# The change-over between two mixers of a hybrid decoder step: work put at other places in the engines' orders

## The chip, the cores and the metric

One core of a Trainium2 chip runs the kernel. Its engines are TensorE (PE), VectorE (DVE), ScalarE (ACT), GpSimd (POOL) and SyncE (SP), which here only issues loads and stores. The metric is the device time of one execution in microseconds; lower is better.

## What is computed

A step of a decoder with two layers, for 512 prompt tokens and 8 sample tokens (520 columns, in two halves of 260). All of it is float32, and each large product is made of three products of high and low parts (high times high, high times low, low times high), so every weight tile needs a "high" copy (ACT) and a "low" remainder (DVE).

```python
h = rmsnorm(y, norm_w[0]);  y = y + ssd_mixer(h)[0]          # layer 0: Mamba-2 SSD, 4 groups, grouped norm, w_out
h = rmsnorm(y, norm_w[1]);  y = y + short_conv_mixer(h)[0]   # layer 1
def short_conv_mixer(h, buf, w_in, conv_w, w_out):
    proj = h @ w_in                                          # (1024, 4 * 2048)
    bg, cg, xin, z = four parts of 2048 columns
    conv, new_buf = causal_dwconv(cg * xin, buf, conv_w)
    return (bg * conv * silu(z)) @ w_out, new_buf
y = rmsnorm(y, final_norm_w)
```

The change-over is the stretch in which the last w_out chunks of layer 0 are added to the residual stream, the sum of squares for layer 1's norm is formed, and layer 1's first tiles are projected.

## The kernel before

The residual stream lies transposed in `xT` (128 x 8 x 520). Each engine runs its own order, written out by hand as a list of calls; semaphores join them. Nothing reorders at run time: an instruction that waits holds all behind it on its engine.

**Layer 0's end on PE.** `out_part(4,'o0',0)` to `out_part(4,'o3',1)` are eight parts of 24 matmuls. They alternate between two PSUM pairs, so each waits (`pair_empty`) until DVE's `residual0` has added the part two before it into `xT` (L1423). Then `first_block` runs four projections of 48 matmuls, IN1 to IN1+3, one for each of z, cg, xin and bg of tile 0 (L2123 again, from `project`). Projection IN1 asks for `hhi` and `hlo` (weighed `xT`, high and low) tile by tile. `token_sums` (L2430) sums the squares over partitions, inside projection IN1+2 before its last two k-tiles. The norm factor r1 is not put into h; it is multiplied in behind the projections on DVE.

**Weights.** SP loads 512 KB chunks into four places of `raw`. `load(n, ...)` waits for the high and low parts of chunk n-2 (same place). `load_part(1,"A22")` and `load_part(1,"A")` use two other places. On ACT, `split(g, what)` makes the high part of the chunk four further on (L624) once PE is done with chunk (g, what); on DVE, `next_low(g, what)` makes the low part (L1238). So `split(3,'l3')` makes chunk (4,'o3'), and `split(4,'o0')` makes chunk IN1, the first of w_in of layer 1.

**The new hidden state.** For each of eight k-tiles: ACT squares `xT` (`x_square`, L915, into `sqb`; tile 0 into `sqs`), makes the weighed high part (`x_weigh0`, L906) and a plain weighed copy (`x_plain`, L1045, into `ybuf`, called h32). DVE makes the low part (`x_low`, L1577) and adds the square up (`add_square`, L1571).

**Layer 1's regular blocks.** `block1(j)` for tiles 1 to 15 makes three of four projections' worth by seven half-size products (P1, P5, P2, P6, P3, P7, P4: 12 matmuls each, L2450) of sums of weight quarters (S1 to S4, DVE `sum_1` to `sum_4`) with sums of h quarters (T1 to T4, `mix`, then `mix_high`, `mix_low`), and two whole chunks Z and G (48 matmuls, L2460). `form_high` (L1121) and `form_low` (L1870) are the high and low parts of these weights. Between products ACT copies PSUM banks away (`snapshot` "s" after P1, "y" after P5, "t" after P6, "u" after P7; L1137); P6 waits for "s", P3 for "y", P7 for "t". `silu_z1(j)` (L1161) is ACT's silu of z, and waits for DVE's product zr (L1959, L1960). L2000 is r2 = -r1 * r1, the first use of the norm factor on DVE.

## Time and profile before

| | us |
|---|---|
| median of 3 runs (892.05 to 894.46) | 893.74 |
| the profiled execution, its own time | 893.7 |
| its span, first to last instruction | 892.0 |
| PE busy | 862.9 (97%) |
| DVE busy | 689.9 (77%) |
| ACT busy | 477.6 (54%) |
| POOL busy | 145.2 (16%) |

Times in the rows are us from the span's start. PE is the engine with the largest share. "idle before <- X" behind a row is the time that the engine stood still ahead of it, and what ended that. Matmuls are pipelined: a row's duration is longer than its distance to the next start.

### The profile page before, as it was taken

To read this page: it belongs to the slowest core of one execution; us is meant where nothing else is said; L and a number is where in the kernel's file an instruction comes from. 1 tells how busy PE (TensorE), PEld (TensorE's weight loads), DVE (VectorE), ACT (ScalarE), POOL (GpSimd) and SP (SyncE) were. 2 spreads that over 40 slices of the span, in tenths; PEclk is the share of its full clock that TensorE was granted. 3 is DMA by queue.
4 is the path that set the end of the run, shared out by engine and by line. 5 is a ranking of instruction groups with operands and counts; after the bars stand their busy time and mean duration, and the time that the engine had idled before them with its cause. 6 is when DMAs were issued, how large, how long until landed. Compare 5 with 4: busy or idle time off the path is not lost.

```text
span 892.0 us, 18650 instructions
## 1 busy us (share of the span) xinstructions
PE 862.9 (97%) x7205; PEld 849.7 (95%) x7205; DVE 689.9 (77%) x1149; ACT 477.6 (54%) x937; POOL 145.2 (16%) x95
## 2 busy tenths in 40 slices
PE   4999999999999999999998999999999999999997
PEld 4999999999999999998998999999999999999996
DVE  4589999969997899987798777777777777774534
ACT  6568668454873576665564444444444444543434
POOL 5404531234143321560000000000000000000000
PEclk9999999999999999999999999999999999999998
DMA  7336636553555436624333333333333333323202
GB/s 173 101 117 196 183 104 194 147 172 118 175 170 163 135 94 212 190 96 126 112 98 96 96 96 95 96 95 96 97 103 104 104 106 104 118 83 110 94 1 96
DMA packets 163023, 108.43 MB, mean 122 GB/s; under 512 B 5000, under 2 KB 155152, under 8 KB 162368
## 3 DMA queue, kind: packets, MB, share of 16 engines
q1 hardware_dynamic: 123876, 76.15, 30.1%
q10 hardware_dynamic: 38756, 30.61, 11.1%
q8 instruction: 58, 0.95, 0.4%
q0 software_dynamic: 304, 0.48, 0.4%
q14 instruction: 29, 0.24, 0.1%
HBM read 95.35 MB, written 12.14 MB: 121 GB/s over the span
## 4 chain that ended last, share of the span: by engine, by line
PE 66%; DVE 13%; issue 4%; ACT 3%; DMA 2%; DVEq 0%; POOLq 0%; POOL 0%; ACTq 0%; SPq 0%
PE pair L2460 19%; PE bank L2450 17%; PE pair L2123 11%; PE pair L2183 6%; PE pair L2393 5%; PE bank L2393 5%; DVE acc L1368 2%; DMA raw<-in_sc_w_in 1%; DVE wlo L1238 1%; DVE ylo L1407 1%; PE bank L2276 1%; PE bank L2261 1%; DVE ybuf L1398 1%; DVE em L1462 1%; PE bank L2293 1%
## 5 line engine op out<-in xcount | busy, mean ns | idle before, releaser
L2123 PE MATMUL pair<-hhi,whi 128*128 128x260 f32 x656 | 135.2, 288 | 0.6 <-DVE acc L1368 0.6
L2123 PE MATMUL pair<-hhi,wlo 128*128 128x260 f32 x656 | 132.5, 284 | 0.0
L2123 PE MATMUL pair<-hlo,whi 128*128 128x260 f32 x656 | 132.2, 283 | 0.0
L2123 PEld LDWEIGHTS pair<-hhi,whi 128*128 128x128 f32 x656 | 101.4, 189 | 2.4 <-DVE acc L1368 1.4
L2123 PEld LDWEIGHTS pair<-hlo,whi 128*128 128x128 f32 x656 | 101.9, 190 | 0.0
L2123 PEld LDWEIGHTS pair<-hhi,wlo 128*128 128x128 f32 x656 | 101.5, 189 | 0.0
L2460 PE MATMUL pair<-hhi,wlo 128*128 128x260 f32 x480 | 96.8, 283 | 0.0
L2460 PE MATMUL pair<-hlo,whi 128*128 128x260 f32 x480 | 96.7, 283 | 0.0
L2460 PE MATMUL pair<-hhi,whi 128*128 128x260 f32 x480 | 96.7, 282 | 0.0
L1121 ACT ACTIVATE whi<-raw 128x1024 fp32r<-128x1024 f32 (+1 forms) x60 | 57.0, 951 | 73.4 <-PE pair L2460 66.4
L624 ACT ACTIVATE whi<-raw 128x1024 fp32r<-128x1024 f32 x60 | 63.1, 1054 | 42.0 <-DMA raw<-in_ssd_w_in 35.6
L1870 DVE TENSOR_TENSOR wlo<-raw,whi 128x1024 fp32r<-128x1024 f32 (+1 forms) x60 | 65.5, 1091 | 23.0 <-ACT whi L1121 22.9
L1238 DVE TENSOR_TENSOR wlo<-raw,whi 128x1024 fp32r<-128x1024 f32 x56 | 70.9, 1274 | 6.9 <-ACT whi L624 6.3
L2460 PEld LDWEIGHTS pair<-hhi,whi 128*128 128x128 f32 x480 | 74.1, 189 | 0.0
L2460 PEld LDWEIGHTS pair<-hhi,wlo 128*128 128x128 f32 x480 | 74.0, 188 | 0.0
L2460 PEld LDWEIGHTS pair<-hlo,whi 128*128 128x128 f32 x480 | 73.8, 188 | 0.0
L539 POOL TENSOR_TENSOR sample<-sample 128x1024 f32<-128x1024 f32 x16 | 48.9, 3059 | 94.1 <-DVE sample L1536 94.1
L1368 DVE SCALAR_TENSOR_TENSOR acc<-pair,colA,acc 128x512 f32<-128x512 f32 (+1 forms) x72 | 54.1, 751 | 6.8 <-ACT acc L751 5.0
L2183 PE MATMUL pair<-yhi,whi 128*128 128x260 f32 x256 | 53.7, 291 | 4.2 <-DVE ylo L1407 2.4
L2450 PE MATMUL bank<-fhi,whi 128*128 128x260 f32 x180 | 51.1, 284 | 2.6 <-ACT sqs L1137 2.6
L2183 PE MATMUL pair<-ylo,whi 128*128 128x260 f32 x256 | 52.1, 285 | 0.0
L2183 PE MATMUL pair<-yhi,wlo 128*128 128x260 f32 x256 | 52.0, 285 | 0.0
(332 smaller groups left out, 2221.9 us busy)
## 6 DMA issues: line engine op xcount, KB each, us to landing
raw<-in_sc_w_in SPq DMA_DIRECT2D x64, 512.0 KB, 5.1
raw<-in_ssd_w_in SPq DMA_DIRECT2D x40, 512.0 KB, 4.0
abc<-a_rows ACTq DMA_DIRECT2D x16, 512.0 KB, 4.3
sample<-in_state_ssm ACTq DMA_DIRECT2D x16, 512.0 KB, 4.3
out_new_ssm_s<-sample ACTq DMA_DIRECT2D x16, 512.0 KB, 5.1
raw<-in_ssd_w_out SPq DMA_DIRECT2D x16, 512.0 KB, 3.9
raw<-in_sc_w_out SPq DMA_DIRECT2D x16, 512.0 KB, 3.8
sample<-bc_rows ACTq DMA_DIRECT2D x4, 1024.0 KB, 6.0
```

Source lines behind the costliest of these rows:

```text
L539: pool.tensor_tensor(tdec, st[:, q % 2, :].rearrange("p (b n) -> p b n", n=NS), bcbc[:, :, 1, :], ALU.mult).then_inc(t2_done, 1)
L624: act.activation(whi[:, slot, :], raw[:, slot % RAW, :], ACT.Copy).then_inc(hi_done, 1)
L1121: act.activation(form_of(whi, j, f), form_src(j, f), ACT.Copy).then_inc(form_hi, 1)
L1238: dve.tensor_tensor(wlo[:, slot, :], raw[:, slot % RAW, :], whi[:, slot, :].bitcast(F32), ALU.subtract).then_inc(lo_done, 1)
L1368: t = dve.scalar_tensor_tensor(acc[:, 0:n], pair[p][:, COL0 - PRE0 + k:COL0 - PRE0 + k + n], cw0(k, tile), acc[:, 0:n], ALU.mult, ALU.add)
L1398: dve.scalar_tensor_tensor(y, y, colB[:, w:w + 1], sqs[:, g, :], ALU.mult, ALU.mult).then_inc(ys_done, 1)
L1870: dve.tensor_tensor(form_of(wlo, j, f), form_src(j, f), form_of(whi, j, f).bitcast(F32), ALU.subtract).then_inc(form_lo, 1)
L2123: mm = pe.matmul(b, w[:, slot, k * P:(k + 1) * P], h[:, k, cols], start=(k == 0 and i == 0), stop=(k == KT - 1 and i == 2))
L2183: mm = pe.matmul(half(p, hb), w[:, slot, k * 256 + part * P:k * 256 + (part + 1) * P], y[:, k, hb * TH:(hb + 1) * TH], start=(k == 0 and i ...
L2393: mm = pe.matmul(bank[2 * i + hb][:, 0:TH], w[:, OUT_SLOT[c % SLOT], kk * 512 + i * P:kk * 512 + (i + 1) * P], y[:, hb * TH:(hb + 1) * TH] ...
L2450: mm = pe.matmul(bank[b][:, 0:TH], form_of(w, j, f)[:, cols], h[:, k, :], start=(first and k == 0 and i == 0), stop=(k == 3 and i == 2), s ...
L2460: mm = pe.matmul(bank[b + hb][:, 0:TH], form_of(w, j, f)[:, k * P:(k + 1) * P], h[:, k, hb * TH:(hb + 1) * TH], start=(k == 0 and i == 0), ...
```

## The change

The number of instructions stays the same; some stand at other places.

- SP: the first two loads of the regular block, A22 and A, are issued behind the first and the second projection chunk, not ahead of all four.
- ACT, layer 0's end: in place of squares in one late group, each k-tile's square follows its weighing, into `thx` for even k and `sqb` for odd k (`square_buf`); the wait of square k for the adds is one step looser. The plain copies of tiles 3 to 7 go to the end, and the `split` calls stand elsewhere.
- DVE, layer 0's end: low parts of w_out's chunks one residual earlier, squares added up as they come, three mixes in a row.
- PE: `token_sums` inside projection IN1+1, not IN1+2.
- ACT and DVE, first block: `mix_high(0)`, `mix_high(2)`, `mix_low(0)` ahead of the norm's roots; in block 1 snapshots "s" and "y" ahead of `silu_z1(1)`.

```diff
@@ SP
-            load_part(1, "A22")
-            load_part(1, "A")
             for m, part in enumerate(PARTS):
                 load(IN1 + m, IN1 + m, w_in1[:, :, part * DI:part * DI + P])
+                if m == 0:
+                    load_part(1, "A22")
+                elif m == 1:
+                    load_part(1, "A")
@@ ACT, x_square
-                if k > 1:
-                    act.wait_ge(xsum_done, 7 * layer + k - 1)
-                act.activation(sqs[:, 0, :] if k == 0 else sqb[:, :], xT[:, k, :], ACT.Square).then_inc(sq_done, 1)
+                if layer == 0 and k > 2:
+                    act.wait_ge(xsum_done, k - 2)
+                elif layer == 1 and k > 1:
+                    act.wait_ge(xsum_done, 7 + k - 1)
+                act.activation(sqs[:, 0, :] if k == 0 else square_buf(layer, k), xT[:, k, :], ACT.Square).then_inc(sq_done, 1)
@@ ACT, block 1
-                silu_z1(j)
+                if j > 1:
+                    silu_z1(j)
                 snapshot(j, "s")
                 snapshot(j, "y")
+                if j == 1:
+                    silu_z1(j)
@@ DVE, layer 0's end (the first of it)
             residual0(3, 'l3', 1)
+            next_low(3, 'l1')
+            next_low(3, 'l2')
             residual0(4, 'o0', 0)
-            next_low(3, 'l1')
+            residual0(4, 'o0', 1)
             x_low(0)
-            residual0(4, 'o0', 1)
-            next_low(3, 'l2')
+            next_low(3, 'l3')
+            x_low(1)
             residual0(4, 'o1', 0)
-            x_low(1)
-            next_low(3, 'l3')
+            add_square(0, 1)
+            next_low(4, 'o0')
             x_low(2)
             residual0(4, 'o1', 1)
@@ PE, first_block
-                    project(IN1 + m, m, ..., None if m else KT, token_sums if m == 2 else None)
+                    project(IN1 + m, m, ..., None if m else KT, token_sums if m == 1 else None)
```

The lines of the kernel are 3 to 8 higher after the change than before: L1238 is L1245, L1423 is L1430, L1577 is L1584, L1571 is L1578, L624 is L629, L915 is L922, L906 is L911, L1045 is L1052, L1121 is L1125, L1137 is L1141, L1161 is L1165.

DVE at layer 0's end, before, from the last residual of (3,'l3') on: `xT` rows are residuals, `wlo` low parts of weights, `hlo` low parts of h.

```order
L1423 TENSOR_TENSOR xT<-xT,pair 128x520 x2
L1238 TENSOR_TENSOR wlo<-raw,whi 128x1024
L1577 SCALAR_TENSOR_TENSOR hlo<-xT,colB,hhi 128x520
L1423 TENSOR_TENSOR xT<-xT,pair 128x520
L1238 TENSOR_TENSOR wlo<-raw,whi 128x1024
L1423 TENSOR_TENSOR xT<-xT,pair 128x520
L1577 SCALAR_TENSOR_TENSOR hlo<-xT,colB,hhi 128x520
L1238 TENSOR_TENSOR wlo<-raw,whi 128x1024
```

The same place after the change:

```order
L1430 TENSOR_TENSOR xT<-xT,pair 128x520
L1245 TENSOR_TENSOR wlo<-raw,whi 128x1024 x2
L1430 TENSOR_TENSOR xT<-xT,pair 128x520 x2
L1584 SCALAR_TENSOR_TENSOR hlo<-xT,colB,hhi 128x520
L1245 TENSOR_TENSOR wlo<-raw,whi 128x1024
L1584 SCALAR_TENSOR_TENSOR hlo<-xT,colB,hhi 128x520
L1430 TENSOR_TENSOR xT<-xT,pair 128x520
L1578 TENSOR_TENSOR sqs<-sqs,sqb 128x520
```

Two low parts moved ahead of the residual of (4,'o0',0), and the residual of (4,'o1',0), the last `xT` row here, moved behind a low part and the second `hlo`.

ACT from the last high part of layer 1's first block on, before: the row `th<-zh` is `silu_z1(1)`, the two rows behind it are snapshots "s" and "y".

```order
L1156 ACTIVATE yhi<-sample 128x1040
L1121 ACTIVATE whi<-raw 128x1024
L1161 ACTIVATE th<-zh 128x520
L1137 ACTIVATE sqs<-bank 128x260
L1137 ACTIVATE yob<-bank 128x260
```

The same place after the change:

```order
L1125 ACTIVATE whi<-sample 128x512
L1125 ACTIVATE whi<-raw 128x1024
L1141 ACTIVATE sqs<-bank 128x260
L1141 ACTIVATE yob<-bank 128x260
L1165 ACTIVATE th<-zh 128x520
```

The two snapshots stand ahead of the silu now.

## Rows read from the trace of the kernel before

**Rows 1.** The page's first part: busy us (share of the span) and instructions.

```profile
PE 862.9 (97%) x7205; PEld 849.7 (95%) x7205; DVE 689.9 (77%) x1149; ACT 477.6 (54%) x937; POOL 145.2 (16%) x95
```

**Rows 2.** Waits of PE, 400 to 480 us: total, times, longest.

```profile
PE bank L2450 <- ACT sqs L1137: 2.6, 1, 2.6
PE pair L2183 <- DVE ylo L1407: 2.0, 1, 2.0
PE pair L2183 <- DVE wlo L1238: 1.1, 1, 1.1
```

**Rows 3.** Windows of PE: length, busy (instructions), granted clock, DMA share, GB/s.

```profile
408.00:411.50 3.50, 3.49 (x17) 0.54 0.00 0
...
475.60:876.00 400.40, 400.40 (x3333) 1.00 0.33 93
```

**Rows 4.** Timeline of PE at the gaps: start, us, operation, count, idle before.

```profile
226.67 1.04 PE L2196 MATMUL bank<-sqs,ones 128*128 128x260 f32 x4
227.55 0.39 PE L2221 MATMUL bank<-turned 128*128 128x128 f32 x2
...
408.01 0.56 PE L2183 MATMUL pair<-yhi,whi 128*128 128x260 f32 x2 [1.99 <-DVE ylo L1407]
...
411.77 0.40 PE L2183 MATMUL pair<-yhi,whi 128*128 128x260 f32 x2
...
426.60 0.40 PE L2183 MATMUL pair<-yhi,wlo 128*128 128x260 f32 x2
428.12 0.47 PE L2183 MATMUL pair<-yhi,whi 128*128 128x260 f32 x2 [1.13 <-DVE wlo L1238]
...
449.54 0.41 PE L2123 MATMUL bank<-hhi,wlo 128*128 128x260 f32 x2
...
451.31 0.40 PE L2123 MATMUL bank<-hlo,whi 128*128 128x260 f32 x2
...
468.25 0.28 PE L2450 MATMUL bank<-hhi,wlo 128*128 128x260 f32 x1
471.16 0.39 PE L2450 MATMUL bank<-fhi,whi 128*128 128x260 f32 x1 [2.63 <-ACT sqs L1137]
...
475.60 0.41 PE L2460 MATMUL pair<-hhi,whi 128*128 128x260 f32 x2
```

**Rows 5.** Timeline of SP: two of its loads.

```profile
414.93 0.37 SPq L377 DMA_DIRECT2D raw<-in_ssd_w_out  x1
...
417.79 0.67 SPq L377 DMA_DIRECT2D raw<-in_sc_w_in  x1
```

**Rows 6.** Chain that ended last, 412 to 456 us: start, us, what.

```profile
417.79 7.05 DMA raw<-in_sc_w_in
...
427.23 0.70 DVE xT L1423
...
445.15 4.00 DMA raw<-in_sc_w_in
```

**Rows 7.** Timeline of ACT at the change-over.

```profile
408.66 1.05 ACT L624 ACTIVATE whi<-raw 128x1024 fp32r<-128x1024 f32 x1
...
418.83 1.06 ACT L624 ACTIVATE whi<-raw 128x1024 fp32r<-128x1024 f32 x1 [1.12 <-DMA raw<-in_ssd_w_out]
...
470.20 0.64 ACT L1161 ACTIVATE th<-zh 128x520 f32<-128x520 f32 x1 [4.78 <-DVE zh L1960]
470.74 0.37 ACT L1137 ACTIVATE sqs<-bank 128x260 f32<-128x260 f32 x1
```

**Rows 8.** Timeline of DVE at the change-over.

```profile
409.61 0.69 DVE L1423 TENSOR_TENSOR xT<-xT,pair 128x520 f32<-128x520 f32 x1
...
449.33 0.70 DVE L1571 TENSOR_TENSOR sqs<-sqs,sqb 128x520 f32<-128x520 f32 x1 [0.17 <-ACT sqb L915]
...
454.34 0.70 DVE L2000 SCALAR_TENSOR_TENSOR sqs<-sqs 128x520 f32<-128x520 f32 x1
...
469.41 0.42 DVE L1959 TENSOR_TENSOR zh<-pair,sqs 128x260 f32<-128x260 f32 x1
```

More of the change, by code:

```diff
@@ L302, in dec_conv, with square_buf @@
             return row[:, SEQ:T]
+        def square_buf(layer, k):
+            return thx[:, :] if layer == 0 and k % 2 == 0 else sqb[:, :]
         def y_tile(g, q):
@@ L1049, in _ @@
             x_weigh0(0)
-            x_plain(0)
-            x_weigh0(1)
-            x_plain(1)
-            split(3, 'l3')
-            x_weigh0(2)
-            x_plain(2)
+            split(3, 'l3')
+            x_weigh0(1)
+            x_square(0, 1)
+            split(4, 'o0')
+            x_weigh0(2)
+            x_square(0, 2)
+            x_plain(0)
             x_weigh0(3)
-            x_plain(3)
+            x_square(0, 3)
+            split(4, 'o1')
             store_state(3, 2)
             store_state(3, 3)
-            split(4, 'o0')
-            x_square(0, 1)
             x_weigh0(4)
-            x_plain(4)
+            x_square(0, 4)
+            x_plain(1)
             x_weigh0(5)
-            x_plain(5)
+            split(4, 'o2')
+            x_square(0, 5)
+            x_plain(2)
             x_weigh0(6)
-            x_plain(6)
-            split(4, 'o1')
+            x_square(0, 6)
             x_weigh0(7)
-            x_plain(7)
-            x_square(0, 2)
-            x_square(0, 3)
-            x_square(0, 4)
-            x_square(0, 5)
-            split(4, 'o2')
+            x_square(0, 7)
             split(4, 'o3')
-            x_square(0, 6)
-            x_square(0, 7)
+            for k in range(3, KT):
+                x_plain(k)
             final_state(3, 3)
@@ L1170, in _ @@
             form_high(1, "Z")
+            mix_high(0)
+            mix_high(2)
             act.wait_ge(stat_mm, GROUPS + 1)
@@ L1175, in _ @@
             load_table(SILU)
-            mix_high(0)
             silu_z1(0)
@@ L1179, in _ @@
             form_high(1, "S1")
+            form_high(1, "S2")
             first_tap1(0)
-            form_high(1, "S2")
-            mix_high(2)
+            mix_high(3)
             form_high(1, "S4")
             form_high(1, "S3")
-            mix_high(3)
             for j in range(1, TILES):
                 form_high(j, "G")
-                silu_z1(j)
+                if j > 1:
+                    silu_z1(j)
                 snapshot(j, "s")
                 snapshot(j, "y")
+                if j == 1:
+                    silu_z1(j)
                 form_high(j, "A22")
@@ L1570, in add_square @@
                     dve.wait_ge(xsum_done, 7 * layer + k - 1)
-                dve.tensor_tensor(sqs[:, 0, :], sqs[:, 0, :], sqb[:, :], ALU.add).then_inc(xsum_done, 1)
+                dve.tensor_tensor(sqs[:, 0, :], sqs[:, 0, :], square_buf(layer, k), ALU.add).then_inc(xsum_done, 1)
             def x_low(k):
@@ L1918, in first_block @@
                 cache_row(0)
+                mix_low(2)
+                weigh_silu(0)
+                form_low(1, "A")
                 dve.wait_ge(proj_done, IN1 + 3)
@@ L1923, in first_block @@
                 dve.tensor_tensor(dec[:, :, PRE1], bank[5][:, SEQ - TH:TH], u[:, SEQ:T], ALU.mult).then_inc(xin_free, 1)
-                weigh_silu(0)
-                form_low(1, "A")
+                mix(3)
                 form_low(1, "S1")
                 conv1(0)
-                mix(3)
+                form_low(1, "S2")
+                mix_low(3)
                 dve.wait_ge(proj_done, IN1 + 4)
@@ L1933, in first_block @@
                 dve.tensor_tensor(yt[:, TH:T], bank[7][:, 0:TH], c2[:, TH:T], ALU.mult).then_inc(bg_free, 1)
-                mix_low(0)
-                form_low(1, "S2")
                 form_low(1, "S4")
-                mix_low(2)
                 form_low(1, "S3")
-                mix_low(3)
             def corner11(j):
@@ L1994, in _ @@
             mix_low(1)
+            form_low(1, "Z")
             dve.wait_ge(xsum_done, 7)
             sum_4(1)
-            form_low(1, "Z")
-            mix(2)
+            mix_low(0)
             dve.wait_ge(rs_done, GROUPS + 1)
@@ L2441, in first_block @@
                         pe.wait_ge(ln_done, GROUPS + 1)
-                    project(IN1 + m, m, bank[2 * m][:, 0:TH], bank[2 * m + 1][:, 0:TH], None if m else KT, token_sums if m == 2 else None)
+                    project(IN1 + m, m, bank[2 * m][:, 0:TH], bank[2 * m + 1][:, 0:TH], None if m else KT, token_sums if m == 1 else None)
             def product(j, what, f, part, b, hi, lo, first):
```

35 lines of the change are left out of this document (17 added, 18 removed).

## The prediction

> **What bounds the kernel now.** Read the busy shares first: TensorE (PE) is busy for 862.9 of 892.0 us [rows 1], so only time in which PE stands idle or runs slowly can be won. Next read whom PE waited for between 400 and 480 us, the stretch that the diff touches: three waits, of 2.6, 2.0 and 1.1 us [rows 2]. From 475.6 to 876 us PE is busy for 400.40 of 400.40 us [rows 3], so whatever PE gains ahead of 475.6 us moves the end by the same amount, as long as nothing later waits.
>
> The price of a gap is best taken from starts, not from idle time. In the steady stretch a matmul takes 400.40 / 3333 = 0.120 us [rows 3], a pair 0.24. The PE timeline [rows 4] then gives:
> - **Gap A**, ahead of out_part(4,'o3',0): the pair at 426.60 makes way at 426.84, the next starts at 428.12: 1.28 us.
> - **Gap B**, at token_sums. Undisturbed, its four passes take 227.55 - 226.67 = 0.88 us. Here the pair at 449.54 makes way at 449.78, and the second pair behind the sums starts at 451.31, so the first at 451.07 in effect: 1.29 - 0.88 = 0.41 us.
> - **Gap C**, ahead of product P6 of the first regular block: 468.25 + 0.12 = 468.37 to 471.16, 2.79 us.
> - A fourth loss, the wait of 1.99 us that ends at 408.01 and the 3.76 us for the 18 matmuls behind it (2.16 at the steady rate), hangs on the group norm and y_low. The diff leaves that order alone.
>
> A, B and C are 4.48 us. A check from the other side: from 408.01 to 475.60 PE issues 8 parts of 24 matmuls, 4 projections of 48, one chunk of 48 and six products of 12, that is 504, 60.5 us at 0.120; with 0.88 for the sums and 1.60 for the slow stretch, 63.0 of 67.6 us, so 4.6 us are lost (the 0.1 more is the refilling of the array behind each gap). I use 4.5.
>
> **The change, part by part.** No instruction is added or removed. What counts is which wait ends last.
>
> *Loads and low parts (gap A).* In the chain [rows 6] DVE's residual add at 427.23 (L1423), which frees the PSUM pair for PE, stands on DVE behind the low part of the first sc_w_in projection chunk. That waits for ACT's high part, and that for the load issued at 417.79, which took 7.05 us: SP issued it behind A22, A and the last ssd_w_out chunk (414.93 [rows 5]). Now both low parts l1 and l2 follow the residual at 409.61 [rows 8], 0.6 us later: the first runs from 410.2 to 411.4, the second to 412.6. The high part of the second is there, ACT having started it at 408.66 for 1.05 us [rows 7]. So the last ssd_w_out chunk is issued at about 411.5 instead of 414.93, and the projection chunk at 412.7 instead of 417.79. The next residual cannot start before 412.5 anyway, when PE ends that part (411.77 + 3 pairs [rows 4]), so the two low parts cost nothing there.
> - ssd_w_out took 3.9 us (414.93 until ACT started on it at 418.83 [rows 5, 7]): now it lands at 415.4. ACT makes its high part from 415.4 to 416.4, ahead of x_weigh0(1), whose input is ready at 416.3, one residual behind PE's 415.4. DVE: x_low(0) to 417.0, low part l3 to 418.1, x_low(1), residual (4,'o1',0) from 418.8 to 419.5. PE wants it at 412.5 + 3 parts of 2.88 = 421.1: 1.6 us of cover.
> - The projection chunk: a lone load took 4.00 us, the one behind three others 7.05 [rows 6]. Landing at 416.7 to 419.7. I take 417, since one chunk stands ahead of it now and not three. High part done at 418.5 (at worst 420.8), low part done at 421.2 (at worst 422.1), x_low(2), residual (4,'o1',1) done at 422.6 (at worst 423.5); PE wants it at 424.0. Then residual (4,'o2',0) at 424.7 to 425.4, against 426.84. Gap A closes: 1.28 us.
> - A22 and A now stand between the projection chunks. Chunk IN1+1 waits for low part l3, so it is issued at 418.2; even at 7.05 us it is there at 425.2, and PE asks for it at 438. IN1+2 and IN1+3 have 20 us. A22 and A are read by the sums, after 428. Each is covered.
> - The same order seen with a rule: A22 was issued 0.4 us behind the ssd_w_out chunk, and this one still took only 3.9 us [rows 5, 7]; a later load took nothing from it. The Trainium skill (DMA: Bandwidth & Descriptors, "Queues, rings and completion order") says that completion is not first-in, first-out per issuing engine. By that rule the projection chunk could end late although A22 now stands behind it, and residual (4,'o1',1) would come at the worst case above; the trace shows no such case.
>
> *Squares (gap B).* With one buffer each square waited for the add before it, and the seventh add ran at 449.33 for 0.70 us [rows 8], 0.25 us too late for PE at 449.78. Now the squares alternate between sqb and thx and follow each x_weigh0, and the last add comes right behind x_low(7). PE ended (4,'o3',1) at 428.12 + 2 x 2.88 = 433.9, now at 432.6; residual, weighing, square, low part and add, each 0.6 to 0.7, are done near 436. PE asks for the sums within projection IN1+1, at 432.6 + 5.8 + 4.3 = 442.7. Cover 6 us; gap B closes: 0.41 us. The plain copies go behind on ACT: the last five, at the residual's 0.7 us each, end near 439.5, so mix(0) starts there instead of earlier; three mixes (1.2 each) and sum_2 end at 443.6. Next on DVE is r2, which needs PE's sums (443.6) and ACT's logs and roots; with two mix_high of 1.0 each ahead of them not before 446. The late copies are covered by that.
>
> *Snapshots (gap C).* P6 waited for snapshot "s" at 470.74, which stood on ACT behind silu_z1(1) at 470.20, and that behind DVE's zr product at 469.41 [rows 7, 8]. DVE reached this so late because from r2 (454.34) on it had 15.1 us of work in a row. Two things are removed. The snapshots go ahead of silu_z1(1). And r2 starts near 447.5 instead of 454.34, since the sums come a projection earlier, with mix_low(0) (1.15 us) done before it; DVE is through by 447.5 + 15.1 - 1.15 = 461.5. PE reaches P6 at 468.37 - 1.28 - 0.41 = 466.7; "s" is taken after P1, at 464, and DVE's S2 and mix_low(0) are ready by 459. Even without the swap the silu would be done at 463.5. Late next is snapshot "t" for P7: silu_z1(1), the high parts A22 and Z (2.3 us together) end by 467.7, P6 at 468.1, "t" at 468.5, P7 at 469.6. Gap C closes: 2.79 us.
>
> **Sum:** 893.7 - 4.5 = 889.2 us. 893.7 is the profiled execution's own time (span 892.0 and 1.7 around it); the median of the runs is 893.74, so nothing is to be shifted.
>
> **The rivals.**
> 1. *A new wait in the output projections.* Residual (4,'o1',0) now stands behind x_low(1), that behind x_weigh0(1), that behind a high part that waits for the ssd_w_out load. If this lands after 417 instead of at 415.4, PE waits. For it: the cover is only 1.4 to 1.6 us at three residuals in a row, and a load took 7.05 us once. Against it: that one had three ahead. It gives back 1 to 2.3 us: 890.2 to 891.5.
> 2. *Gap C closes by half.* If DVE stays late, P7 waits for "t" behind a silu at 470.2 and two high parts, 1.4 us: 890.6. Against it: 5 us of cover.
> 3. *The clock.* Behind the 1.99 us gap the granted clock was 0.54 [rows 3], so mostly at the 1.2 GHz level; behind the 2.63 us gap PE kept its pace (36 matmuls in the 4.44 us from 471.16 to 475.60 [rows 4]), that of 2.4 GHz. A gap of that size costs 1.60 us or nothing. The kept gap may come without it, 887.6, or a small new gap may bring it, 890.8. The Trainium skill (TensorE: Matmul & The Clock Gate, "Part 1: The HAM clock gate") has the gate observe PE independently of when the kernel began; by that rule the same gap may cost in one run and not in the next.
> 4. *Slower than before.* The chain of rival 1 with a very late load: each us of landing beyond 417.0 is one us of PE. Break-even with 893.7 is a landing at 421.5; slower by over 0.3% needs 424.2, 12.7 us after issue, where the slowest load shown took 7.05. At 425 the time would be 897.2.
> 5. *It does nothing*, if PE's path holds something not seen behind these gaps: 893.7. Against it: the 504 matmuls account for all but these 4.6 us.
>
> **How the numbers follow.** Forecast 889.2 (its own range 888.2 to 890.1): 0.66. Rival 1: 0.14. Rival 2: 0.05. Rival 3: 0.08. Rival 4: 0.03. Rival 5: 0.04. The range runs from the lower end of rival 3 to just above rival 1, 887.6 to 891.8, and leaves out under 0.2. A difference of 0.3%, 2.7 us, is about what a measurement of this kernel can tell from no change; the line is 891.0. Faster: 0.66 x 0.95, half of rival 1, nearly all of 2 and 3: 0.80 less a little for scatter, 0.79. Slower 0.03, same 0.18.
>
> **What the changed profile would show.** PE's waits between 400 and 480 us hold only the one of 2.0 us for y_low; the projection chunk is issued near 412.7; the sums stand near 442.7 with no gap; P6 follows P2 directly near 466.7; chunk "G" starts near 471.1 instead of 475.60. I am wrong if PE waits for the xT adds between 421 and 424, or if the low clock stands at another place.

## The result, and the profile after

| | before | after |
|---|---|---|
| median beside each other on one chip, 11 executions each | 892.26 us (891.64 to 895.54) | 888.01 us (885.11 to 890.57) |
| ratio | | 0.9938 [0.9924, 0.9952] |
| profiled execution: its time / its span | 893.7 / 892.0 us | 885.1 / 883.4 us |

The change makes the kernel faster by 0.62%: 0.0062 x 892.26 = 5.5 us, with the interval 4.3 to 6.8 us. The forecast was 4.5 us off 893.7, so 889.2. The direction and the waits that closed were forecast rightly; the gain by the ratio is 1 us larger, though its interval still holds the 4.5. The ratio times the 892.26 of the same chip is 886.7 us, under the lower end of 887.6; the measured median itself, 888.01, lies inside the range. The two medians alone would give a ratio of 0.9952 (4.25 us). The median of before is an unsteady number, because its eleven times fall into two groups (six from 891.64 to 892.26, five from 893.74 to 895.54). The means, 893.26 and 887.91 us, give 0.9940. One execution of e1 below took 1696.29 us, in the slow state, and is in none of the numbers.

The first thing to see is the page's busy list of the changed kernel, against [rows 1]: PE has nearly the same busy time (861.0 against 862.9) in a span 8.6 us shorter.

```profile
span 883.4 us, 18649 instructions
## 1 busy us (share of the span) xinstructions
PE 861.0 (97%) x7205; PEld 848.5 (96%) x7205; DVE 687.1 (78%) x1149; ACT 477.1 (54%) x937; POOL 146.8 (17%) x95
```

PE's waits of the changed kernel between 390 and 480 us, against [rows 2]: of three one is left, the one that the diff does not touch.

```profile
engine line waited for: us in total, times, longest us
PE pair L2190 <- DVE ylo L1414: 2.0, 1, 2.0
```

PE's timeline of the changed kernel (columns: start, duration, engine, line, operation, idle before), at the places of [rows 4]: the last matmul before the kept gap and the first behind it; token_sums; the step into product P6; and the start of chunk G.

```profile
403.48 0.40 PE L2190 MATMUL pair<-yhi,wlo 128*128 128x260 f32 x2
405.89 0.47 PE L2190 MATMUL pair<-yhi,whi 128*128 128x260 f32 x2 [2.01 <-DVE ylo L1414]
...
438.98 0.82 PE L2437 MATMUL bank<-sqs,ones 128*128 128x260 f32 x3
...
462.80 0.28 PE L2457 MATMUL bank<-hhi,wlo 128*128 128x260 f32 x1
462.92 0.28 PE L2457 MATMUL bank<-fhi,whi 128*128 128x260 f32 x1
...
467.26 0.41 PE L2467 MATMUL pair<-hhi,whi 128*128 128x260 f32 x2
```

P6 starts 0.12 us behind the matmul before it, where 2.9 us lay between them [rows 4]. Windows of the changed kernel behind the kept gap and over the steady stretch (columns: stretch, its length, busy time of each engine, then the granted clock, the DMA share and GB/s):

```profile
405.89:409.49 3.60, 3.60 (x30) 3.60 (x31) 3.60 (x6) 1.68 (x3) 0.00 (x0) 1.00 0.00 0
467.30:868.00 400.70, 400.70 (x3336) 400.70 (x3335) 277.44 (x479) 168.20 (x287) 0.00 (x0) 1.00 0.33 93
```

Behind the same 2.0 us gap PE now runs at a granted clock of 1.00, the 2.4 GHz level, where before it was 0.54 [rows 3].

**Where the 8.6 us between the two spans are.** I cut each record at PE starts: up to the first matmul behind the 2.0 us gap; from there to chunk G of the first regular block; from there to the last output projection; the rest. (Starts from the PE timelines, before rounding, so that a difference of the printed rows can be 0.01 off; G is at 475.60 before [rows 4] and 467.26 after.)

| record | to the end of the 2.0 us gap | from there to chunk G | G to last projection | rest | low clock behind these gaps |
|---|---|---|---|---|---|
| before | 408.01 | 67.59 | 402.62 | 13.75 | the 2.0 us gap |
| after | 405.89 | 61.38 | 402.62 | 13.48 | neither |

- The second column fell by 6.21 us. The slow 18 matmuls behind the gap cost 1.60 by the prediction's reckoning from [rows 3]; between records of the changed kernel below, the difference is 1.53 us. Without it 4.68 remain, where the three gaps had been sized at 4.48 and the cross-check by 504 matmuls had said 4.6.
- The first column fell by 2.12 us, in a stretch that the change leaves alone. It is scatter: in the records below it ends anywhere from 405.5 to 409.0, for kernels of either order.
- The steady stretch is the same to 0.01 us, so what PE gains ahead of G does move the end.

So one profile against another (8.6 us) says half as much again as the change is worth. The timed executions say 5.5 us (4.3 to 6.8). The question for the experiments is the 1 us between that and the gaps, of which the interval alone does not say that it is there.

### The profile page after: what moved, and what is told of

Its sections match the earlier page's. It is cut to its first block, busy times and chain, and to the rows that moved or that the text cites. A ratio compares the mean times of both kernels' runs of the same rounds, so it can differ in the third digit from the quotient of the medians.

```text
span 883.4 us, 18649 instructions
## 1 busy us (share of the span) xinstructions
PE 861.0 (97%) x7205; PEld 848.5 (96%) x7205; DVE 687.1 (78%) x1149; ACT 477.1 (54%) x937; POOL 146.8 (17%) x95
## 4 chain that ended last, share of the span: by engine, by line
PE 74%; DVE 8%; issue 3%; ACT 2%; DMA 1%; POOLq 0%; DVEq 0%; POOL 0%; ACTq 0%
PE pair L2467 20%; PE bank L2457 17%; PE pair L2130 14%; PE pair L2190 8%; PE pair L2400 5%; PE bank L2400 5%; DVE acc L1375 2%; PE bank L2130 1%; PE bank L2283 1%; PE bank L2268 1%; DVE wlo L1245 1%; DVE ybuf L1405 1%; DVE em L1469 1%; PE bank L2030 1%; DMA abc<-a_rows 1%
## 5 line engine op out<-in xcount | busy, mean ns | idle before, releaser
L1125 ACT ACTIVATE whi<-raw 128x1024 fp32r<-128x1024 f32 (+1 forms) x60 | 57.1, 951 | 78.5 <-PE pair L2467 71.5
L629 ACT ACTIVATE whi<-raw 128x1024 fp32r<-128x1024 f32 x60 | 63.2, 1053 | 40.2 <-DMA raw<-in_ssd_w_in 35.2
L1245 DVE TENSOR_TENSOR wlo<-raw,whi 128x1024 fp32r<-128x1024 f32 x56 | 70.9, 1273 | 1.9 <-ACT whi L629 1.2
L2457 PE MATMUL bank<-flo,whi 128*128 128x260 f32 x180 | 51.0, 283 | 0.0
```

Of the source, the lines that this page charges most:

```text
L629: act.activation(whi[:, slot, :], raw[:, slot % RAW, :], ACT.Copy).then_inc(hi_done, 1)
L1125: act.activation(form_of(whi, j, f), form_src(j, f), ACT.Copy).then_inc(form_hi, 1)
L1245: dve.tensor_tensor(wlo[:, slot, :], raw[:, slot % RAW, :], whi[:, slot, :].bitcast(F32), ALU.subtract).then_inc(lo_done, 1)
L2457: mm = pe.matmul(bank[b][:, 0:TH], form_of(w, j, f)[:, cols], h[:, k, :], start=(first and k == 0 and i == 0), stop=(k == 3 and i == 2), s ...
```

## The experiments

Three theories for what lies beyond the gaps. **Theory 1:** low clocks behind gaps; with fewer and shorter gaps fewer executions get one. **Theory 2:** the change removed something that the prediction had not seen. **Theory 3:** the scatter ahead of 408 us alone. Beside them each step of the prediction is tried for itself. All were timed in three sets (e, f and g), each set on one chip beside the kernel before. (The expectation of f1 calls scatter inside the change-over theory 2, that of g1 calls "no drop, only scatter" theory 3.)

| kernel | median us | ratio to before | us from the first matmul behind the 2.0 us gap to G | low clock behind the 2.0 us gap / gap C |
|---|---|---|---|---|
| e1 changed, again | 887.52 | 0.9924 [0.9899, 0.9950] | 62.91 | yes / no gap |
| f1 changed, again | 887.58 | 0.9942 [0.9921, 0.9964] | 62.94 | yes / no gap |
| e2 changed, no swap | 888.55 | 0.9934 [0.9912, 0.9956] | 62.92 | yes / no gap |
| e3 before + swap | 891.11 | 0.9972 [0.9959, 0.9985] | 65.67 | yes / no |
| e4 changed, old loads | 889.19 | 0.9950 [0.9930, 0.9969] | 63.66 | yes / no gap |
| f4 changed, sums late | 888.39 | 0.9950 [0.9932, 0.9969] | 61.45 | no / no gap |
| f3 before + low parts | 893.79 | 1.0008 [0.9992, 1.0023] | 68.02 | yes / yes |
| g2 the same, again | 892.36 | 0.9999 [0.9982, 1.0015] | 66.50 | no / yes |
| g1 before, again | 893.30 | 1.0008 [0.9992, 1.0025] | 66.83 | no / yes |
| f2 changed + early y tile | 886.36 | 0.9930 [0.9909, 0.9951] | (see there) | no / no gap |
| g3 changed, loads later | 888.00 | 0.9951 [0.9933, 0.9968] | 62.90 | yes / no gap |
| g4 both | 886.66 | 0.9938 [0.9915, 0.9960] | (see there) | no / no gap |

### The changed kernel again (e1, f1)

No edit.

> The changed kernel again, beside the kernel before on one chip, for the part of the gain that the sum does not explain (about 5.5 us measured, 4.5 us summed). Theory 1: the gaps A, B and C are worth 4.5 us, and the rest is TensorE's clock: fewer stretches at the low level in the changed kernel. Then the two kernels' executions, sorted by their mean granted clock, differ by 4.5 us at equal clock (a difference of 0.001 of mean clock is 0.9 us), and the changed kernel's mean clock is higher by about 0.001. Theory 2: the rest lies in a fourth gap that closed too; then the two differ by 5.5 us at equal clock, and a PE timeline aligned matmul by matmul shows a further step between 400 and 480 us. Theory 3: the rest is scatter of the stretch before 400 us, where both kernels have the same orders; then the gain here is anything from 3.5 to 6.5 us.

> The changed kernel once more, beside the kernels of this call. Theory 1 (the three gaps give 4.7 us, and beyond them only the clock drop behind the 2.0 us gap at layer 0's end comes and goes): 0.5 to 0.7% under before, and the stretch from that gap to the chunk G of the first block at 61.4 us without a low clock in it or 62.9 us with it, never between. Theory 2 (scatter of the whole program hides a part of the change elsewhere): that stretch varies by itself, by more than 0.2 us around the two values.

Measured: 62.91 and 62.94 us from the gap's end to G, where the first record had 61.38. The one difference is the clock behind the gap: the PE row and window of f1, the window's fourth number being the granted clock.

```profile
407.29 0.48 PE L2190 MATMUL pair<-yhi,whi 128*128 128x260 f32 x2 [2.00 <-DVE ylo L1414]
```

```profile
408.10:411.50 3.40, 3.40 (x19) 0.51 0.02 5
```

The same gap, in the same kernel: 0.51 here, 1.00 there. It costs 1.53 to 1.56 us or nothing, and in all seven records of the changed order with the 2.0 us gap (after, e1, f1, e2, e4, f4, g3) the stretch had one of these two values (in e4 with the wait shown below on top), never one between. Theory 2 finds no place in the change-over: before and after differ there by the gaps and by low clocks. Theory 3 is true of single records (405.9 to 408.4 us for the first column), but it touches kernels of both orders alike, so it can't move a ratio of medians by itself.

### The swap of the snapshots (e2, e3)

In the changed kernel the swap undone, and in the kernel before the swap alone:

```diff
@@ e2: ACT, block 1 of the changed kernel
-                if j > 1:
-                    silu_z1(j)
+                silu_z1(j)
                 snapshot(j, "s")
                 snapshot(j, "y")
-                if j == 1:
-                    silu_z1(j)
@@ e3: the same edit, the other way, in the kernel before
```

> The changed kernel with one part undone: in block 1, silu_z1(1) stands ahead of the snapshots s and y again. My theory: the early norm factor alone brings DVE to zr by 463 us, so the silu is done before P1 ends and the swap is worth nothing: within 0.3 us of the changed kernel, PE with no wait ahead of P6. Rival: the swap is what closed gap C: 2.8 us slower than the changed kernel, P6 waiting for snapshot s behind the silu.

> The kernel before with the swap alone: snapshots s and y ahead of silu_z1(1). Nothing else moved. Theory: P6 no longer waits, but P7 then waits for snapshot t, which stands behind the silu (zr at about 470 us) and two high parts, for 1.4 to 1.7 us: a gain of 1.2 to 1.4 us on the kernel before. Rival: if the snapshot order was the cause of the whole gap C, the gain is 2.8 us and no wait is left at P7.

e2: 62.92 us against 62.91 with the swap. Once the norm factor comes early the swap is worth nothing, as the prediction's step on gap C said ("even without the swap"). e3: alone, it moves the wait from P6 to P7. PE's waits of e3, and PE and ACT around P7:

```profile
PE pair L2186 <- DVE ylo L1410: 2.0, 1, 2.0
PE bank L2453 <- ACT sqs L1137: 1.2, 1, 1.2
PE pair L2186 <- issue: 0.6, 1, 0.6
```

```profile
470.08 0.28 PE L2453 MATMUL bank<-hhi,wlo 128*128 128x260 f32 x1
471.57 0.39 PE L2453 MATMUL bank<-fhi,whi 128*128 128x260 f32 x1 [1.22 <-ACT sqs L1137]
```

```profile
469.14 0.64 ACT L1161 ACTIVATE th<-zh 128x520 f32<-128x520 f32 x1 [2.70 <-DVE zh L1963]
469.69 1.56 ACT L1121 ACTIVATE whi<-raw 128x512 fp32r<-128x512 f32 x2
471.15 0.36 ACT L1137 ACTIVATE sqs<-bank 128x260 f32<-128x260 f32 x1
```

The chain of rival 2 is there as it was written: silu, two high parts, snapshot "t", P7. It costs 471.57 - 470.08 - 0.12 = 1.37 us, where the prediction said 1.4. The swap alone wins half of gap C, 1.42 us; the other 0.5 us of e3's gain in this record is a smaller gap A (0.6 against 1.1 us in the list of waits), which the swap does not touch.

The timed executions of e3 gain more than the 1.2 to 1.4 us that I expected: 0.28%, 2.5 us (1.3 to 3.7). Their mean granted clock is 0.9928, against 0.9908 for before in the same set. So the wait of 2.6 us that became one of 1.2 us seems to have taken its low clock with it. None stands behind the 1.2 us wait in this record. It is the first sign of what the section on the low parts shows.

### The sums one projection later (f4)

```diff
@@ PE, first_block of the changed kernel
-    project(..., token_sums if m == 1 else None)
+    project(..., token_sums if m == 2 else None)
```

> The changed kernel with PE's token sums back inside projection IN1+2, one projection (5.8 us) later. The prediction said that gap C closes because the norm factor comes a projection earlier, and that the swap of the snapshots is not needed. It also said that DVE would be through its 15.1 us behind r2 by 461.5, 5 us ahead of PE; with the sums 5.8 us later it would be through near 467 and the snapshot s, which now stands ahead of the silu, does not wait for that chain. So theory (either edit alone holds gap C closed for P6): no wait for s, at most 0.5 us at P7 for t, and a time within 0.6 us of the changed kernel. Rival (the early sums carry gap C by themselves): a wait of 1 to 1.5 us at P7 as in the swap alone, and the ratio to before 0.0015 higher than the changed kernel's.

61.45 us, against 61.38 of the record that likewise had no low clock; no wait but the kept one. So gap C is held closed twice over: by the swap with late sums (f4), and by the early sums without the swap (e2). With neither, in the kernel before, it is open. The time, 888.39 against 887.58 us of the changed kernel in the same set, has overlapping intervals.

### The order of the loads (e4, g3)

e4 puts A22 and A back ahead of the projection chunks; g3 puts both behind the second one.

```diff
@@ e4: SP, the changed kernel
+            load_part(1, "A22")
+            load_part(1, "A")
             for m, part in enumerate(PARTS):
                 load(IN1 + m, IN1 + m, ...)
-                if m == 0:
-                    load_part(1, "A22")
-                elif m == 1:
-                    load_part(1, "A")
@@ g3: SP, the changed kernel
-                if m == 0:
-                    load_part(1, "A22")
-                elif m == 1:
-                    load_part(1, "A")
+                if m == 1:
+                    load_part(1, "A22")
+                    load_part(1, "A")
```

> The changed kernel with one part undone: SP issues A22 and A ahead of the projection chunks again. All low parts, squares and sums stay where the change put them. Theory (loads are served in the order of issue, about 1.9 us each once under way): the first projection chunk lands at 420.9 instead of 417, DVE's residual (4,'o1',1) is late and PE waits 0.8 us at about 424: 0.8 us slower than the changed kernel. Rival (loads share the engines evenly, so the order of issue does not matter): no difference, no wait. Second rival: the last ssd_w_out chunk ahead of them is slowed too, and PE waits for residual (4,'o1',0) as well: 2 us or more slower.

> The changed kernel, with the loads A22 and A both issued behind the second projection chunk, so that nothing is issued behind the first one for 4 to 5 us. In five records of the changed order that first chunk took 5.1, 5.1, 5.4, 5.9 and 6.3 us from its issue until ACT used it, with A22 issued 0.4 us behind; in the record before a load by itself took 4.0. Theory (loads in flight share the engines, later ones take from earlier ones): 4.0 to 4.8 us, ACT waits for it less, and nothing moves at PE, since PE does not wait there: within 0.3 us of the changed kernel in the stretch from the 2.0 us gap to chunk G (61.4 or 62.9). Rival (later loads take nothing): still 5.1 to 6.3 us.

e4: 63.66 us, 0.75 more than e1, with the same low clock. The place is out_part(4,'o2',1); ACT's high parts of e4 show what was late.

```profile
423.83 0.40 PE L2188 MATMUL pair<-yhi,wlo 128*128 128x260 f32 x2
424.74 0.48 PE L2188 MATMUL pair<-yhi,whi 128*128 128x260 f32 x2 [0.51 <-issue]
```

```profile
415.47 1.06 ACT L627 ACTIVATE whi<-raw 128x1024 fp32r<-128x1024 f32 x1 [0.63 <-DMA raw<-in_ssd_w_out]
420.87 1.06 ACT L627 ACTIVATE whi<-raw 128x1024 fp32r<-128x1024 f32 x1 [3.15 <-DMA raw<-in_sc_w_in]
```

ACT waited 3.15 us for the projection chunk. In the changed kernel the loads and the high parts stand as follows; before they are [rows 5, 7].

```profile
409.41 0.37 SPq L380 DMA_DIRECT2D raw<-in_ssd_w_out  x1
410.55 0.37 SPq L380 DMA_DIRECT2D raw<-in_sc_w_in  x1
410.96 0.58 SPq L407 DMA_DIRECT2D raw<-in_sc_w_in  x1
```

```profile
412.87 1.06 ACT L629 ACTIVATE whi<-raw 128x1024 fp32r<-128x1024 f32 x1 [0.46 <-DMA raw<-in_ssd_w_out]
415.62 1.06 ACT L629 ACTIVATE whi<-raw 128x1024 fp32r<-128x1024 f32 x1 [0.55 <-DMA raw<-in_sc_w_in]
```

From issue to use the chunk took 5.07 us (410.55 to 415.62), not the 4.3 that the prediction took. In the other records of this order it took at most 5.05 (e1, where ACT did not wait for it), 5.36 (f1), 5.86 (f4), 6.26 (e2) and, in f2, 6.60 us. With nothing issued behind it it was at most 4.96 us in g3, where ACT did not wait for it, and 4.80 in g4. What stands ahead of it costs PE 0.75 us (e4). What stands behind it makes its landing later and less even, if two records against six can say so; PE gains nothing by that in g3: 62.90 us. The prediction cited the Trainium skill (DMA: Bandwidth & Descriptors, "Queues, rings and completion order") for the rule that completion is not first-in, first-out per issuing engine; by that rule a chunk may end late although A22 stands behind it. The trace agrees: each load lands in sixteen parts, and in f2 (6.60 us) the first part of A22 landed at 418.04 us, before the chunk's last at 419.07. It was so in e2 and f4 too, while in the records with 5.05 to 5.36 us A22's first part came behind the chunk's last.

### The low parts alone (f3, g2) and the kernel before again (g1)

```diff
@@ f3 and g2: DVE at layer 0's end, the kernel before
             residual0(3, 'l3', 1)
+            next_low(3, 'l1')
+            next_low(3, 'l2')
             residual0(4, 'o0', 0)
-            next_low(3, 'l1')
             x_low(0)
             residual0(4, 'o0', 1)
-            next_low(3, 'l2')
```

> The kernel before, with one edit of the change alone: the low parts of the w_out chunks l1 and l2 stand ahead of the residual of (4,o0,0), where DVE waits for PE anyway. The step of the prediction on gap A says that with it SP issues the last w_out chunk and the first projection chunk 2 to 5 us earlier. The projection chunk, still behind A22 and A, should land 2 to 5 us earlier too, so that gap A (1.28 us) shrinks to 0 to 0.9 us, and PE is 0.4 to 1.3 us earlier from there to the end; gaps B and C stay. Ratio to before 0.9985 to 1. Rival (loads queue behind A22 and A whatever their issue time): gap A stays within 0.2 us of 1.28.

> The same kernel as the low parts alone, for a second record. Gap A should again be gone (PE from the first matmul behind the 2.0 us gap to gap C 1.0 to 1.3 us sooner than before), gap C again whole. Theory 1: its mean clock is that of the kernel before (0.990 to 0.991), since both gaps stand, and its time 0 to 1.3 us under before; the tie measured first was scatter. Rival (something slows PE when gap A is closed, and gives the 1.1 us back each time): a tie with before again, with a lower mean clock or a low clock behind gap C again.

> The kernel before once more, for a second record of its change-over. In the profile of the low parts alone a low clock stood behind gap C (2.6 us, ahead of product P6) as well as behind the 2.0 us gap at layer 0's end. Theory 1 (a gap of 2 to 3 us brings a low clock in a part of the executions, worth 1.5 us; the change took gap C away and with it this chance, which the prediction priced at nothing): mean clock of the executions near 0.991, two or three thousandths under the changed kernel's, and from the first matmul behind layer 0's 2.0 us gap to chunk G 66.0 to 69.2 us, in steps of about 1.5 us, according to how many of the two gaps are followed by a low clock. Theory 3 (no such drop in the kernel before; the rest of the gain is scatter of the program ahead of 408 us): 67.6 or 66.1 us, and mean clocks like those of the changed kernel.

These three bear most on the cause. f3 did close gap A (0.24 us left of 1.28), and yet tied with before. Its record shows one reason: PE behind gap C, and the windows of f3 behind gap C and behind the 2.0 us gap (columns: length, PE busy and matmuls, granted clock).

```profile
468.18 0.28 PE L2450 MATMUL bank<-hhi,wlo 128*128 128x260 f32 x1
471.09 0.39 PE L2450 MATMUL bank<-fhi,whi 128*128 128x260 f32 x1 [2.63 <-ACT sqs L1137]
```

```profile
471.80:475.20 3.40, 3.40 (x19) 0.50 0.28 77
410.40:413.80 3.40, 3.40 (x18) 0.50 0.03 8
```

A granted clock of 0.50, the 1.2 GHz level, stands behind gap C too. The first record of before had none there, and I had read it as a property of the gap:

```profile
471.20:474.60 3.40, 3.40 (x28) 1.00 0.09 23
```

In the repeated kernel before, g1, it is the other way round: none behind the 2.0 us gap, one behind gap C. PE around gap C, and the windows, of g1:

```profile
465.89 0.28 PE L2450 MATMUL bank<-hhi,wlo 128*128 128x260 f32 x1
468.79 0.59 PE L2450 MATMUL bank<-fhi,whi 128*128 128x260 f32 x1 [2.62 <-ACT sqs L1137]
469.17 0.42 PE L2450 MATMUL bank<-flo,whi 128*128 128x260 f32 x1
...
474.68 0.40 PE L2460 MATMUL pair<-hhi,whi 128*128 128x260 f32 x2
```

```profile
468.80:472.00 3.20, 3.20 (x15) 0.50 0.08 22
408.00:411.50 3.50, 3.50 (x30) 1.00 0.02 5
```

From P6's start to G the three records with the low clock took 5.89 us (g1: 474.68 - 468.79), 5.93 (f3) and 5.94 (g2); the first record of before took 4.44 [rows 4]. So a low clock behind gap C costs 1.5 us, and it stood in three of the four records that have gap C whole (one of the two of the kernel before, both with the low parts alone). In the ten records in which gap C is closed or halved, none stood there. g2:

```profile
466.60:470.00 3.40, 3.40 (x18) 0.50 0.21 56
405.60:409.00 3.40, 3.40 (x29) 1.00 0.00 0
```

The four records add up: from the gap's end to P6 63.15 us (before); less 1.04 for gap A is 62.11 (f3: 62.08); less 1.53 for the clock as well is 60.58 (g2: 60.56). g1 had a smaller gap A by itself, 0.63 us by the PE rows:

```profile
424.91 0.40 PE L2183 MATMUL pair<-yhi,wlo 128*128 128x260 f32 x2
425.78 0.48 PE L2183 MATMUL pair<-yhi,whi 128*128 128x260 f32 x2 [0.47 <-issue]
```

The unprofiled executions carry only a mean clock. Each low stretch of 3.4 us at half pace lowers it by 1.7 / 890 = 0.0019. Over the three sets the kernel before has a mean of 0.9909 and 893.0 us (60 executions); the changed kernel, with its first measurement, 0.9934 and 887.7 us (22 executions); the low parts alone 0.9902 (24 executions). That is 1.3 low stretches fewer in the changed kernel. At 1.5 us each they would be 2 us, more than the 1 us to be explained; but low stretches stand also near 19, 46 and 882 us in records of either order, where PE has idle time and they may cost less, so the mean clock gives the sign and not the size. Theory 1's expectation on this point (two or three thousandths) held; theory 3's (no difference in clocks) did not.

The expectation of e1 asked for the difference at equal mean clock. I put one straight line of time on mean clock through the same 60 and 22 executions, with a step between the kernels. The step is 3.7 us (2.9 to 4.5), of 5.3 us between the means. By theory 1 it should be 4.5 us, or 3.8 with the smaller gap A of g1, and by theory 2 it should be 5.5. This bears theory 1 out and speaks against theory 2. The line falls by 0.66 us for each 0.001 of clock, less than the 0.9 that e1 expected, which fits low stretches that cost little at the ends of the program.

That f3 and g2 measured no gain (ratios 1.0008 and 0.9999) where the trace shows gap A smaller is only in part explained: gap A in the kernel before is 1.28 us in one record and 0.63 in the other, so about 0.7 us is to be won on average, which the intervals of about 0.0015 (1.3 us) do not exclude for g2; f3's lower end, 0.9992, allows 0.7. At equal mean clock, by the same kind of line, the low parts alone are 0.4 us faster (0.2 slower to 1.1 faster). What g2's expectation set against theory 1 is not excluded: a tie again, with a low clock behind gap C again, is what came. Closing gap A may make the low clock behind gap C more frequent (two of two records, one of two without it); four records can't tell that from chance.

### The early y tile (f2, g4)

What the change left is the 2.0 us gap. In f2 tile 0 of the last group's normed y goes into tile 7 of the old h (free since projection (3,'z3')), so that its parts need not wait for PE; g4 adds g3's loads.

```diff
+        def yg_slot(g, q):
+            if g == 3 and q == 0:
+                return hhi[:, 7, :], hlo[:, 7, :]
+            return yhi[:, q, :], ylo[:, q, :]
@@ ACT y_high and DVE y_low
-                if g > 0:
+                if g == 3 and q == 0:
+                    wait_ge(proj_done, NUMBER[3, "z3"] + 1)
+                elif g > 0:
@@ DVE, layer 0's end
             norm_scale(3, 0)
             norm_scale(3, 1)
+            y_low(3, 0)
             norm_scale(3, 2)
             norm_scale(3, 3)
-            y_low(3, 0)
@@ ACT, layer 0's end: copy_tails() behind the four y_high, not behind the first
@@ (left out here: PE, the high and low parts and their operands take their tile from yg_slot)
```

> The changed kernel, with tile 0 of the last group's normed y written into the last tile of the old h, so that its high and low part need not wait until PE has ended the out projection before them, and DVE makes the first low part between its norm scalings. The one gap of 2.0 us that the change left should then break up: in the rows of after DVE's four scalings take 2.77 us and four low parts 2.52 us in a row, and PE ran dry 1.4 us before the first low part. PE would start out_part(4,o0,0) some 1.4 us earlier after the end of the part before it, and then wait twice about 0.5 us for DVE at tiles 1 and 2: the end of that part 0.3 to 0.6 us earlier. Theory 1 (a gap of that length sometimes brings a low clock, worth 1.5 us): with the gap cut, no low clock there, and the kernel is 0.3 to 2 us faster than the changed kernel, ratio to it 0.998 to 0.9995. Rival (the low clock comes whatever the gap is, or the shorter gaps bring it as well): a low clock stretch stands at 405 to 410 us all the same, and only 0.3 to 0.6 us are won.

> The kernel with the early y tile 0 and this later place of A22 and A. The early tile alone broke the 2.0 us gap into 0.79 and 0.99 us without a low clock behind it, but PE waited 0.78 us at out_part(4,o2,1), as the projection chunk took 6.6 us to land. Theory: with 4.0 to 5.0 us that wait is gone, and no low clock stands near 410 us: 0.8 us better than the early tile alone and 1 to 2 us better than the changed kernel, ratio to before 0.990 to 0.9925. Rival (the landing is as late as before, by other traffic): the wait of 0.8 us stays and the kernel ties with the changed one.

f2, PE: the gap is broken in two, as expected, and a new wait of rival 1's kind stands at out_part(4,'o2',1). The second fence is ACT's high part of the projection chunk.

```profile
406.55 0.48 PE L2201 MATMUL pair<-hhi,whi 128*128 128x260 f32 x2 [0.79 <-ACT yhi L798]
...
408.50 0.48 PE L2201 MATMUL pair<-yhi,whi 128*128 128x260 f32 x2 [0.99 <-ACT yhi L798]
...
423.17 0.48 PE L2201 MATMUL pair<-hhi,whi 128*128 128x260 f32 x2 [0.78 <-issue]
```

```profile
419.15 1.06 ACT L634 ACTIVATE whi<-raw 128x1024 fp32r<-128x1024 f32 x1 [1.89 <-DMA raw<-in_sc_w_in]
```

g4, SP's issue and ACT's use of the chunk (4.80 us apart), and the window over both halves of the gap:

```profile
412.25 5.20 SPq L385 DMA_DIRECT2D raw<-in_sc_w_in  x2
```

```profile
417.05 1.06 ACT L633 ACTIVATE whi<-raw 128x1024 fp32r<-128x1024 f32 x1 [0.25 <-DMA raw<-in_sc_w_in]
```

```profile
406.30:413.00 6.70, 5.70 (x46) 1.00 0.09 26
```

Measured from the last matmul before the gap to G (403.59 to 467.26 in the first record after: 63.67 us), g4 took 63.74 us: the 0.3 to 0.6 us that I expected at the end of out_part(4,'o0',0) did not come. DVE's eight operations in a row (four scalings, four low parts, 5.3 us) still end last, and splitting PE's wait doesn't shorten them. (The rows name ACT's high part ahead of 408.50 us in f2. The one that PE asks for there was done at 406.5; DVE's low part was the last, at 408.35.) The wait at out_part(4,'o2',1) is gone in g4, as its theory said. No low stretch stood behind the split gap in either record, where 8 of the 12 records with the 2.0 us gap whole had one. That may be what is won, but at a share of 8 in 12 two records without one come about once in nine times by luck. The mean clocks don't settle it either: 0.9937 for f2 and for f1, 0.9943 for g4 against 0.9933 for g3. The medians are 886.36 (f2) and 886.66 us (g4), 1.2 us under the changed kernel (887.58) and 1.3 us under g3 (888.00) of the same sets; the intervals overlap, so that it is faster than the changed kernel is likely, not shown. Both beat the kernel before: 0.9930 and 0.9938. For g4 I had expected 0.990 to 0.9925 and 0.8 us less than f2; it is level with f2.

## Where the prediction was right, and which step failed

The three gaps closed as forecast, by the waits that it named. Two terms of the line "893.7 - 4.5 = 889.2" failed: gap C priced at 2.79 us without the low clock behind it, and the base of 893.7 with "nothing is to be shifted".

- **What bounds the kernel, and the price of gaps by starts.** Right. From G to the last projection PE took 402.62 us in every record up to 0.02, and the change-over lost 4.68 us beside the clock, with 4.48 (4.6 by the cross-check) forecast. Rival 5 is out. The cross-check's "refilling of the array" is a name that no row shows; the rows show only that the first pair behind a gap takes some 0.07 us longer to its next start than the pace (0.31 against 0.24 behind the 2.0 us gap of the changed kernel).
- **Gap A.** Closed, but by less cover than forecast. The projection chunk landed at 5.1 us, not 4.3, after issue; DVE's residual (4,'o1',1), from DVE rows of the changed kernel,

```profile
417.29 1.22 DVE L1245 TENSOR_TENSOR wlo<-raw,whi 128x1024 fp32r<-128x1024 f32 x1
418.43 0.75 DVE L1584 SCALAR_TENSOR_TENSOR hlo<-xT,colB,hhi 128x520 fp32r<-128x520 f32 x1
419.10 0.69 DVE L1430 TENSOR_TENSOR xT<-xT,pair 128x520 f32<-128x520 f32 x1
```

  is done at 419.8, and PE asks at 405.89 + 5 x 2.88 = 420.3: 0.5 us of cover, where I had 1.4. At 6.26 us of landing PE still did not wait (e2), at 6.60 it did (f2), at 7.26 with the old loads it lost 0.75 (e4). Rival 1 had the right kind of mechanism, at a price of 1 us and more where 0.7 to 0.9 was measured, but a place one residual too early, at (4,'o1',0), where the ssd_w_out load came in 3.5 us. And gap A itself was 0.63 us in the second record of before: the term of 1.28 was the larger of two values. It was too large by some 0.3 us on average, against the clock that was left out, so it is luck that the sum of 4.5 is closer to the gain than its terms are.
- **Gap B.** Right: token_sums at 438.98, with 442.7 forecast, less 3.65 for the earlier start and the missing low clock 439.05, and no gap.
- **Gap C.** Closed as said, by either edit alone (e2, f4). r2 started 1.4 us later than I had it (447.5 less 3.65 is 443.85), and 5 us of cover took that up:

```profile
445.23 0.69 DVE L2007 SCALAR_TENSOR_TENSOR sqs<-sqs 128x520 f32<-128x520 f32 x1
```

  What failed is **the size of this term**. "Gap C closes: 2.79 us" priced the gap without a clock, since in the one record that I had PE kept its pace behind it. In three of four records it did not, and then the gap costs 2.79 + 1.5 us (P6 to G in 5.89 to 5.94 us, where the first record had 4.44).
- **Rival 3** said of the clock that a gap of that size costs 1.60 us or nothing, and used it for the kept gap and for a new one, each as a shift of the result; it left out that a removed gap takes its low clock with it. The step should have been, as an estimate from these records: gap C 2.79 + 1.5 x its share (0.5 by the two records of before, 0.75 by all four) = 3.5 to 3.9, gap A 0.63 to 1.28, gap B 0.41: 4.6 to 5.6 us. Measured: 5.5 (4.3 to 6.8). The prediction cited the Trainium skill (TensorE: Matmul & The Clock Gate, "Part 1: The HAM clock gate") for a gate that observes PE independently of when the kernel began. By that rule the same gap may cost in one run and not in the next, and the trace agrees: the 2.0 us gap brought a low clock in 8 of 12 records, gap C in 3 of 4.
- **The base.** "Nothing is to be shifted" leaned on a median of three. These three are among the eleven executions whose median is 892.26 us, so the difference is scatter. Of the 2.5 us between 889.2 and the ratio's 886.7, 1.5 come from this and 1.0 from the gain, for which the clock is the likely cause. With the base of 892.26 the range would have held 886.7.
- **Open:** how much of the 1.0 us is the clock and how much the scatter of the measurement, since the interval of the gain holds 4.5 us too. The mean clock says that there is a difference, the records say where it can stand, and neither gives its size to better than some 0.5 us. Open too: 0.3 us at the end. The rest behind the last projection is 13.75 and 13.80 us in the two records of before and 13.44 to 13.48 in all others, f3 and g2 included, whose order there is that of before; so I don't claim it for the change. And four records are few for a share of 0.75. Gap B was never closed alone.

## What to carry to other kernels

A gap on PE can have two prices: its length, and the low clock that stands behind it in a part of the executions (here 1.5 us behind gaps of 2.0 and 2.6 us, more than gaps A and B cost). When a gap goes, count both; when it only becomes shorter or is split, the second may go by itself (three records here, so not shown). Read the clock behind each gap in several records before taking "none" for its property, and cut the records at PE starts: here one pair of profiles differed by 8.6 us, of which 4.7 were the gaps.

Of a load that stands on a chain with half a microsecond of cover, ask what is in flight with it and by how much its landing varies (here 4.8 to 6.6 us for the same 512 KB), not what it took once.

## What the runs showed of the hardware that I had not expected

- The same gap in the same program is followed by a granted clock of 0.50 in one execution and 1.00 in the next: 2.0 us gaps in 8 of 12 records, 2.6 us gaps in 3 of 4; by these few records the longer gap is not clearly the surer one. The low windows shown have 15 matmul rows in 3.2 us and 18 or 19 in 3.4, where 28 or 29 stand in 3.4 us otherwise, and each low stretch cost 1.5 us. Gaps of 0.8 and 1.0 us had none behind them (two records), nor had the 1.2 us gap of e3.
- The 405 us ahead of the change-over vary by 3.5 us between records (405.5 to 409.0) with the order of instructions unchanged, which is more than gaps B and C together (3.20).
